# Attention scores on TensorE as three 64-row products, the two heads of a pair on the two halves of the array

## The chip, the cores and the metric

The kernel runs on one core of one Trainium2 chip. The metric is the time of one execution on the device, in microseconds (us), as the median of several runs. The profile and the trace are of one further execution. Engines are named as in the profile: PE is TensorE (PEld its weight loads), DVE is VectorE, ACT is ScalarE, POOL is GpSimd, SP is SyncE, which here only issues transfers.

## The reference

One decoder layer on x of 512 tokens by 1024 channels, in float32. What matters here is the attention part:

```
h    = rmsnorm(x, g_norm) * (1 + scale) + shift          # scale, shift, gate from silu(c) @ w_ada
proj = h @ w_in                                          # 1024 -> 4096: q k v z_attn | b_g c_g h_c z_conv
q, k = rope(q, positions), rope(k, positions)            # 8 heads of 64; halves t1, t2 of 32:
                                                         #   [t1*cos - t2*sin, t2*cos + t1*sin]
score = q @ k.T * 64 ** -0.5, causal inside blocks of 256, earlier blocks in full
y_attn = softmax(score) @ v
y_conv = b_g * conv3(c_g * h_c)
y     = concat(rmsnorm(y_attn) * silu(z_attn), rmsnorm(y_conv) * silu(z_conv)) @ w_out
out   = rmsnorm(x + gate * y, g_final)
```

With 512 tokens there are two blocks, so the selection of blocks takes every past block, and the scores are plain causal attention.

## The kernel before

**Precision.** Each float32 factor is split into a high part of fewer bits (`float32r`) and a low part, the rest. A product is three TensorE products, high by low, low by high, high by high, added in PSUM (`mm3`, lines 982 to 985). The high part is a copy on ACT, the low part a subtraction, on POOL for the weights (line 567), on DVE for q, k, v and the probabilities.

**Staging.** After the head of the program (normalised x, then q and k of head pair 0, v of all heads and C of channel group 0), the input projection goes on in 25 *units* of 128 output channels each (the list `UNITS`: H0, B0, Q1, K1, ZC0, ZA0, C1, H1, ...). A unit is 24 matmuls of 512 columns (`unit`). It writes bank n % 2 of PSUM, n its place in the list, so unit n waits until the result of unit n - 2 has been read (`emptied`): for Q and K this is the semaphore `rope_m`, which DVE raises when the products of the rotary step are done; for B it is `y_conv`, raised by `conv_out` on DVE (line 778). Between units stands the attention of one of the four head pairs p: the scores (`score`), the transposed probabilities (`transpose_probs`, ten 128x128 transposes for a head) and the product with v (`values`). Each engine has its work in an order that is written out by hand at the end of its block; semaphores tie the engines together.

**Rotary step.** The 128 channels of a Q or K unit are laid out by the host as first halves of both heads, then second halves, so `rope` on DVE is four operations: q by cos (line 730), two products of 64 rows with the crosswise sine (lines 731, 732), and the sum (line 734), which gives `rq` or `rk`.

**Scores.** For head h of the pair, `qs[:, h]` holds the 64 high rows of q and the 64 low rows side by side in 128 rows, and `kd_hi[:, h]`, `kd_lo[:, h]` hold the rows of k twice. The rows that lie in the wrong place are moved by 12 transfers a pair on the SP queue (`other_rows`, `double_q`, `double_k`). Two matmuls over 128 rows, by `kd_lo` and by `kd_hi`, then give all four partial products (lines 1090, 1091). The scores of one head take 1280 columns (four query tiles of 384, 128, 512 and 256 columns, `S_ORDER`), at banks 2 to 4 (`SB`). Both heads use the same place in turn. So `score(p, 0)` stands ahead of one unit and `score(p, 1)` behind it, and the second waits for `row_min`, DVE's last read of the first. The transposed probabilities go to banks 5 to 7 (`TB`).

**DVE around it.** `least(p, h)` (line 796) takes the scores from PSUM, adds the mask and finds the row minima (the scores are negated); ACT then takes exponentials (line 388), DVE divides by the sum (`normalise`, line 806), PE transposes, ACT copies (`pt_hi`, line 394), DVE subtracts (`probs_low`, line 812), and PE does `values`. In between DVE does the convolution (`conv_taps` lines 761 to 771, `conv_out` line 778) and the modulation vectors (line 671).

Of the kernel before, what the change touches and what calls it, by code (L numbers as in the profile page):

```python
# [4 lines left out]
F32 = mybir.dt.float32  # L5
F32R = mybir.dt.float32r
# [4 lines left out]
P = 128  # L11
# [33 lines left out]
def build(nc, x, c, pos, prm_d, ada_d, whead_d, wslots_d, gfin_d, out):  # L45
# [10 lines left out]
    SB, TB = 2 * BANK, 5 * BANK  # L56
# [6 lines left out]
    with ExitStack() as ctx:  # L63
# [35 lines left out]
        qs = sb("qs", [2, S], F32R)  # L99
# [4 lines left out]
        q_lo = sb("q_lo", [S], F32R)  # L104
        base = cursor[0]
        kd_hi = sb("kd_hi", [2, S], F32R)
        om = at("om", base, [2, BANK])
        base = cursor[0]
        kd_lo = sb("kd_lo", [2, S], F32R)
        h32 = at("h32", base, [2, S])  # L110
# [68 lines left out]
        dup_q, dup_k = sem("dup_q"), sem("dup_k")  # L179
# [46 lines left out]
        def _(sp):  # L226
# [25 lines left out]
            def other_rows(dst, src, h, done):  # L252

                for a in (0, 64):
                    to, of = a + 32 * (1 - h), a + 32 * h
                    sp.dma_start(dst[to:to + 32, h, :].bitcast(F32), src[of:of + 32, :].bitcast(F32)).then_inc(done, 16)
# [7 lines left out]
            def double_k(p):  # L264
                sp.wait_ge(qk_lo, 3 * p + 3)
                for kd in (kd_hi, kd_lo):
                    for h in range(2):
                        other_rows(kd, kd[:, h, :], h, dup_k)

            for n in range(NSLOT):  # L270
                load_raw(KT + n, wslots_d[n], D)
                if n in (5, 10, 16, 21):
                    double_q((5, 10, 16, 21).index(n))
                if n in (5, 10, 17, 22):
                    double_k((5, 10, 17, 22).index(n))
# [16 lines left out]
        def _(act):  # L292
# [58 lines left out]
            def q_high(p):  # L351
                act.wait_ge(rope_r, 2 * p + 1)
                act.wait_ge(scores, 6 * p)
                for h in range(2):
                    nc.scalar.activation(qs[:, h], rq[:, :], ACT.Copy, scale=-(HD ** -0.5)).then_inc(q_split, 1)

            def k_high(p):
                act.wait_ge(rope_r, 2 * p + 2)
                act.wait_ge(scores, 6 * p)
                for h in range(2):  # L360
                    nc.scalar.activation(kd_hi[:, h], rk[:, :], ACT.Copy).then_inc(k_split, 1)
# [116 lines left out]
            for i in range(2):  # L478
                act.wait_ge(gate_bc, i + 1)
# [826 lines left out]
```

## Time and profile before

| what | value |
|---|---|
| median of 3 runs | 290.88 us (290.7 to 291.0) |
| the profiled execution, its own time | 290.17 us |
| its span in the profile | 288.1 us |
| PE busy | 269.2 us (93% of the span), 1300 matmuls |
| PEld busy | 223.8 us (78%) |
| DVE busy | 198.9 us (69%) |
| ACT busy | 141.5 us (49%) |
| POOL busy | 113.5 us (39%) |
| granted TensorE clock | 0.993 of full over the span |

The own time of the profiled execution is 2.1 us more than its span, and 0.7 us under the median of the three runs. Busy shares are averages over the whole span; how full an engine is in one stretch has to be read from the trace. Matmul ends in the trace are modelled and overlap the next matmul, so the time that a matmul costs is read from start to start.

### The profile page before, as it was taken

To read this page: it belongs to the slowest core of one execution; us is meant where nothing else is said; L and a number is where in the kernel's file an instruction comes from. 1 tells how busy PE (TensorE), PEld (TensorE's weight loads), DVE (VectorE), ACT (ScalarE), POOL (GpSimd) and SP (SyncE) were. 2 spreads that over 40 slices of the span, in tenths; PEclk is the share of its full clock that TensorE was granted. 3 is DMA by queue.
4 is the path that set the end of the run, shared out by engine and by line. 5 is a ranking of instruction groups with operands and counts; after the bars stand their busy time and mean duration, and the time that the engine had idled before them with its cause. 6 is when DMAs were issued, how large, how long until landed. Compare 5 with 4: busy or idle time off the path is not lost.

```text
span 288.1 us, 3732 instructions
## 1 busy us (share of the span) xinstructions
PE 269.2 (93%) x1300; PEld 223.8 (78%) x1300; DVE 198.9 (69%) x348; ACT 141.5 (49%) x239; POOL 113.5 (39%) x72
## 2 busy tenths in 40 slices
PE   5479999999999999999999999999999979999990
PEld 1358888888888888888888887888888858888880
DVE  4798888699989976788998947623945621304564
ACT  5755355349058833764535254647367574302332
POOL 2400002444534433290461352055086799902321
PEclk9999999999999999999999999999999999999997
DMA  5999944394712462076352203253232518100113
GB/s 192 395 419 417 392 162 146 117 404 126 210 59 73 118 197 88 0 269 243 110 146 74 75 1 102 91 137 144 76 106 78 205 50 305 61 0 2 74 73 146
DMA packets 12260, 43.81 MB, mean 152 GB/s; under 512 B 2129, under 2 KB 2129, under 8 KB 10834
## 3 DMA queue, kind: packets, MB, share of 16 engines
q1 hardware_dynamic: 12242, 43.58, 42.6%
q8 instruction: 10, 0.16, 0.2%
q14 instruction: 8, 0.07, 0.1%
HBM read 38.33 MB, written 2.10 MB: 140 GB/s over the span
## 4 chain that ended last, share of the span: by engine, by line
PE 82%; DMA 4%; ACT 4%; POOL 3%; issue 3%; DVE 2%; SPq 1%; POOLq 0%; ACTq 0%; DVEq 0%
PE ps L983 19%; PE ps L985 18%; PE ps L984 18%; PE ps L1032 5%; DMA xt<-in_x 3%; PE ps L1116 3%; PE ps L1108 2%; PE ps L1045 2%; PE ps L1051 2%; PE ps L1043 2%; PE ps L1091 2%; PE ps L1090 2%; POOL yc_lo L583 2%; PE ps L1049 2%; PE ps L1009 1%
## 5 line engine op out<-in xcount | busy, mean ns | idle before, releaser
L567 POOL TENSOR_TENSOR w_lo<-raw,w_hi 128x1024 fp32r<-128x1024 f32 x29 | 73.7, 2549 | 124.9 <-ACT w_hi L321 124.9
L983 PE MATMUL ps<-h_lo,w_hi 128*128 128x512 f32 x200 | 78.9, 395 | 0.0
L985 PE MATMUL ps<-h_hi,w_hi 128*128 128x512 f32 x200 | 78.0, 390 | 0.0
L984 PE MATMUL ps<-h_hi,w_lo 128*128 128x512 f32 x200 | 77.9, 389 | 0.0
L985 PEld LDWEIGHTS ps<-h_hi,w_hi 128*128 128x128 f32 x200 | 37.6, 188 | 8.0
L984 PEld LDWEIGHTS ps<-h_hi,w_lo 128*128 128x128 f32 x200 | 37.6, 188 | 7.2
L983 PEld LDWEIGHTS ps<-h_lo,w_hi 128*128 128x128 f32 x200 | 37.6, 188 | 7.2
L671 DVE CUSTOM_DVE_ANT_0 mod_junk<-ada,c_bc 128x1024 f32<-128x1024 f32 x22 | 33.4, 1519 | 1.5 <-DVE acc L671 0.6
L388 ACT ACTIVATE probs<-probs,rmin 128x384 f32<-128x384 f32 (+3 forms) x32 | 17.6, 552 | 31.5 <-DVE rmin L796 31.4
L321 ACT ACTIVATE w_hi<-raw 128x1024 fp32r<-128x1024 f32 x29 | 30.1, 1050 | 4.1 <-DMA raw<-in_wslots 4.1
L806 DVE TENSOR_SCALAR probs<-probs,prec 128x384 f32<-128x384 f32 (+3 forms) x32 | 21.4, 733 | 0.3
L944 DVE TENSOR_TENSOR om<-ps,gate 128x512 f32<-128x512 f32 (+1 forms) x9 | 5.7, 629 | 20.7 <-PE ps L985 20.7
L529 ACT ACTIVATE sq_junk<-x 128x512 f32<-128x512 f32 (+1 forms) x9 | 5.3, 585 | 27.5 <-DVE x L946 27.5
L796 DVE CUSTOM_DVE_ANT_0 probs<-mask,ps 128x384 f32<-128x384 f32 (+3 forms) x32 | 13.7, 484 | 4.5 <-PE ps L1091 4.5
L343 ACT ACTIVATE h<-ps,sh,gs 128x512 f32<-128x512 f32 x8 | 6.2, 779 | 20.6 <-DVE sh L680 20.0
L983 PE MATMUL ps<-w_lo,yc_hi 128*128 128x512 f32 (+1 forms) x36 | 13.8, 382 | 1.9 <-POOL yc_lo L583 1.9
L812 DVE TENSOR_TENSOR pt_lo<-ps,pt_hi 128x1280 fp32r<-128x1280 f32 x8 | 11.9, 1487 | 4.1 <-ACT pt_hi L394 4.1
L394 ACT ACTIVATE pt_hi<-ps 128x1280 fp32r<-128x1280 f32 x8 | 9.9, 1238 | 8.3 <-PE ps L1108 8.3
L985 PE MATMUL ps<-w_hi,yc_hi 128*128 128x512 f32 (+1 forms) x36 | 13.3, 371 | 0.0
L984 PE MATMUL ps<-w_hi,yc_lo 128*128 128x512 f32 (+1 forms) x36 | 13.3, 370 | 0.0
L985 PE MATMUL ps<-wa_hi,ya_hi 128*128 128x512 f32 (+1 forms) x36 | 13.2, 367 | 0.0
L984 PE MATMUL ps<-wa_hi,ya_lo 128*128 128x512 f32 (+1 forms) x36 | 13.2, 366 | 0.0
(150 smaller groups left out, 508.5 us busy)
## 6 DMA issues: line engine op xcount, KB each, us to landing
raw<-in_wslots SPq DMA_DIRECT2D x33, 512.0 KB, 3.3
ada<-in_ada SPq DMA_DIRECT2D x11, 1024.0 KB, 9.1
raw<-in_whead SPq DMA_DIRECT2D x8, 448.0 KB, 7.2
xt<-in_x SPq DMA_DIRECT2D x4, 512.0 KB, 5.6
x<-in_x SPq DMA_DIRECT2D x4, 512.0 KB, 6.9
out<-x SPq DMA_DIRECT2D x4, 512.0 KB, 2.7
ada<-in_ada SPq DMA_DIRECT2D x2, 512.0 KB, 7.3
qs<-q_lo SPq DMA_DIRECT2D x16, 64.0 KB, 2.0
```

Of the source, the lines that this page charges most:

```text
L321: nc.scalar.activation(slot_place(n)[0], src[:, :], ACT.Copy).then_inc(s_hi, 1)
L388: nc.scalar.activation(probs[h][:, a:a + w], probs[h][:, a:a + w], ACT.Exp, scale=-1.0, bias=rmin[:, e:e + 1], accum_out=psums[:, e:e + 1] ...
L394: nc.scalar.activation(pt_hi[:, :], ps[:, TB:TB + TRI], ACT.Copy).then_inc(p_hi, 1)
L567: nc.gpsimd.tensor_tensor(lo, src[:, :], hi.bitcast(F32), ALU.subtract).then_inc(s_lo, 1)
L671: dve.tensor_tensor_reduce(mod_junk[:, :], src[:, two, :], c_rows, 1.0, 0.0, ALU.mult, ALU.add, acc[:, j, two:two + 1]).then_inc(mod_step, 1)
L796: dve.tensor_tensor_reduce(probs[h][:, a:a + w], mask[:, S - w:S], ps[:, SB + a:SB + a + w], 1.0, 3.0e38, ALU.add, ALU.min, rmin[:, e:e + ...
L806: ins = nc.vector.tensor_scalar(probs[h][:, a:a + w], probs[h][:, a:a + w], prec[:, e:e + 1], None, ALU.mult)
L812: nc.vector.tensor_tensor(pt_lo[:, :], ps[:, TB:TB + TRI], pt_hi[:, :].bitcast(F32), ALU.subtract).then_inc(p_lo, 1)
L983: nc.tensor.matmul(o, a_hi, b_lo, start=start, stop=False)
L984: nc.tensor.matmul(o, a_lo, b_hi, start=False, stop=False)
L985: return nc.tensor.matmul(o, a_hi, b_hi, start=False, stop=stop)
L1032: nc.tensor.matmul(o, a_hi, b_hi, start=(j == 0), stop=False)
```

## The change

The layout of the channels of Q and K stays as the reference has it, head 0 in rows 0 to 63 and head 1 in rows 64 to 127, so no rows need to be moved. `q2[:, 0]` and `q2[:, 1]` are the high and low parts of q, `k2` the same of k. A head's scores are three products over its 64 rows, low by high, high by low, high by high. The matmuls of the two heads alternate: rows 0 to 63 and rows 64 to 127 of the array, to different PSUM banks (2 to 4, and 5 to 7, where the transposed probabilities also go). The built program gives them arrays of 64 rows by 128 columns at row 0 and row 64, where all other matmuls have the array of 128 by 128. The 12 transfers a pair are gone, and so is the second copy of each high part on ACT and the second subtraction for k on DVE. The rotary step now takes its halves from blocks of 32 rows, four products in place of two. Both heads are scored at one place, where `score(p, 0)` was. `transpose_probs` waits until both heads' scores have been read. `gate_rows`, which uses banks 5 and 6, moves from behind unit H2 to behind `values(2, 1)`.

```diff
-    SB, TB = 2 * BANK, 5 * BANK
+    SB, TB = [2 * BANK, 5 * BANK], 5 * BANK
...
-            def double_q(p):
-                sp.wait_ge(q_split, 2 * p + 2)
-                sp.wait_ge(qk_lo, 3 * p + 1)
-                for h in range(2):
-                    other_rows(qs, q_lo, h, dup_q)
...
             def q_high(p):
                 act.wait_ge(rope_r, 2 * p + 1)
                 act.wait_ge(scores, 6 * p)
-                for h in range(2):
-                    nc.scalar.activation(qs[:, h], rq[:, :], ACT.Copy, scale=-(HD ** -0.5)).then_inc(q_split, 1)
+                nc.scalar.activation(q2[:, 0], rq[:, :], ACT.Copy, scale=-(HD ** -0.5)).then_inc(q_split, 1)
...
                 nc.vector.tensor_tensor(m1[:, :], bank(b), cos_t[:, :], ALU.mult)
-                nc.vector.tensor_tensor(m2[0:64, :], bank(b, p0=64, p1=128), sin_t[64:128, :], ALU.mult)
-                nc.vector.tensor_tensor(m2[64:128, :], bank(b, p0=0, p1=64), sin_t[0:64, :], ALU.mult).then_inc(rope_m, 1)
+                for r in range(0, P, 32):
+                    o = r ^ 32
+                    ins = nc.vector.tensor_tensor(m2[r:r + 32, :], bank(b, p0=o, p1=o + 32), sin_t[o:o + 32, :], ALU.mult)
+                ins.then_inc(rope_m, 1)
...
             def k_low(p):
-                dve.wait_ge(k_split, 2 * p + 2)
+                dve.wait_ge(k_split, p + 1)
                 dve.wait_ge(rope_r, 2 * p + 2)
-                for h in range(2):
-                    nc.vector.tensor_tensor(kd_lo[:, h], rk[:, :], kd_hi[:, h].bitcast(F32), ALU.subtract
-                                            ).then_inc(qk_lo, 1)
+                nc.vector.tensor_tensor(k2[:, 1], rk[:, :], k2[:, 0].bitcast(F32), ALU.subtract).then_inc(qk_lo, 1)
...
-            def score(p, h):
-                pe.wait_ge(dup_q, 64 * p + 64)
-                pe.wait_ge(dup_k, 128 * p + 128)
-                if h:
-                    pe.wait_ge(row_min, 8 * p + 4)
-                elif p:
+            def score(p):
+
+                pe.wait_ge(qk_lo, 2 * p + 2)
+                if p:
                     pe.wait_ge(y_attn, 2 * p)
+                    pe.wait_ge(p_lo, 2 * p)
                 else:
                     pe.wait_ge(rope_m, 2)
-                    pe.wait_ge(v_lo, 2)
+                    pe.wait_ge(v_lo, TT)
+                    pe.wait_ge(c_copy, 1)
...
-                    nc.tensor.matmul(o, qs[:, h, t], kd_lo[:, h, 0:w], start=True, stop=False)
-                    ins = nc.tensor.matmul(o, qs[:, h, t], kd_hi[:, h, 0:w], start=False, stop=True)
-                    if n:
-                        ins.then_inc(scores, 1)
+                    for term, (a, b) in enumerate(((1, 0), (0, 1), (0, 0))):
+                        for h in range(2):
+                            rows = slice(HD * h, HD * h + HD)
+                            o = ps[:, SB[h] + S_AT[i]:SB[h] + S_AT[i] + w]
+                            ins = nc.tensor.matmul(o, q2[rows, a, t], k2[rows, b, 0:w], start=(term == 0), stop=(term == 2))
+                            if n and term == 2:
+                                ins.then_inc(scores, 1)
 
             def transpose_probs(p, h):
                 pe.wait_ge(p_norm, 2 * p + h + 1)
-                if p == 0 and h == 0:
-                    pe.wait_ge(v_lo, TT)
-                    pe.wait_ge(c_copy, 1)
-                elif h == 0:
-                    pe.wait_ge(p_lo, 2 * p)
-                    if p == 2:
-                        pe.wait_ge(gate_ok, 2)
+                pe.wait_ge(row_min, 8 * p + 8)
...
             unit("Q1")
-            score(0, 0)
+            score(0)
             unit("K1")
-            score(0, 1)
             unit("ZC0")
             transpose_probs(0, 0)
```

PE's order before, from the last matmul of unit Q1 to the first of K1: eight matmuls for head 0 (`ps` is PSUM, `qs`, `kd_lo`, `kd_hi` the split factors).

```order
L985 MATMUL ps<-h_hi,w_hi_53 128x512
L1090 MATMUL ps<-kd_lo,qs 128x384 [waits rope_m,v_lo,dup_k,dup_q]
L1091 MATMUL ps<-kd_hi,qs 128x384
L1090 MATMUL ps<-kd_lo,qs 128x128
L1091 MATMUL ps<-kd_hi,qs 128x128
L1090 MATMUL ps<-kd_lo,qs 128x512
L1091 MATMUL ps<-kd_hi,qs 128x512
L1090 MATMUL ps<-kd_lo,qs 128x256
L1091 MATMUL ps<-kd_hi,qs 128x256
L983 MATMUL ps<-h_lo,w_hi_54 128x512 [waits y_conv,s_lo]
```

The same place in the change: 24 matmuls of 64 rows for both heads, and the waits for the transfers are one for the low parts.

```order
L957 MATMUL ps<-h_hi,w_hi_53 128x512
L1067 MATMUL ps<-k_81,q_74 128x384 [waits v_lo,c_copy,rope_m,qk_lo]
L1067 MATMUL ps<-k_81,q_74 128x384 x5
L1067 MATMUL ps<-k_81,q_74 128x128 x6
L1067 MATMUL ps<-k_81,q_74 128x512 x6
L1067 MATMUL ps<-k_81,q_74 128x256 x6
L955 MATMUL ps<-h_lo,w_hi_54 128x512 [waits y_conv,s_lo]
```

Head 0's scores moved nowhere; head 1's eight matmuls, which stood behind K1, are gone from there. Unit K1 still waits for `y_conv`.

DVE's order before, `conv_out(0)`, the rotary step of Q1 and the start of `least(0, 0)` (`m_70`, `m_71` are the two addends of the rotary step; an ISA row is the min operation or its read-out):

```order
L778 TENSOR_TENSOR yc<-yc,ps 128x512 [waits unit_out,tap_ok]
L730 TENSOR_TENSOR m_70<-ps,cos_t 128x512 [waits q_split,unit_out]
L731 TENSOR_TENSOR m_71<-ps,sin_t 64x512
L732 TENSOR_TENSOR m_71<-ps,sin_t 64x512
L734 TENSOR_TENSOR rq<-m_70,m_71 128x512 [waits rope_m]
L796 ISA probs_92,rmin<-mask,ps 128x384 [waits scores,mask_ok]
```

The same in the change:

```order
L750 TENSOR_TENSOR yc<-yc,ps 128x512 [waits unit_out,tap_ok]
L703 TENSOR_TENSOR m_70<-ps,cos_t 128x512 [waits q_split,unit_out]
L706 TENSOR_TENSOR m_71<-ps,sin_t 32x512 x4
L709 TENSOR_TENSOR rq<-m_70,m_71 128x512 [waits rope_m]
L768 ISA probs_90,rmin<-mask,ps 128x384 [waits scores,mask_ok]
```

Two instructions of 64 rows have become four of 32 rows of the same length, at the same place; the order of DVE's steps is otherwise kept.

PE's order before, from the end of unit ZC0 over the transposes of head 0 to unit ZA0:

```order
L984 MATMUL ps<-h_hi,w_lo_61 128x512
L985 MATMUL ps<-h_hi,w_hi_55 128x512
L1108 MATMUL ps<-ident,probs_92 128x128 [waits c_copy,v_lo,p_norm]
L1108 MATMUL ps<-ident,probs_92 128x128 x9
L983 MATMUL ps<-h_lo,w_hi_56 128x512 [waits rope_m,s_lo]
```

And in the change:

```order
L956 MATMUL ps<-h_hi,w_lo_61 128x512
L957 MATMUL ps<-h_hi,w_hi_55 128x512
L1078 MATMUL ps<-ident,probs_90 128x128 [waits row_min,p_norm]
L1078 MATMUL ps<-ident,probs_90 128x128 x9
L955 MATMUL ps<-h_lo,w_hi_56 128x512 [waits rope_m,s_lo]
```

The transposes of head 0 now wait for `row_min` of both heads.

## Rows read from the trace of the kernel before

**Rows 1.** The page: busy time of each engine over the span.
```profile
PE 269.2 (93%) x1300; PEld 223.8 (78%) x1300; DVE 198.9 (69%) x348; ACT 141.5 (49%) x239; POOL 113.5 (39%) x72
```

**Rows 2.** The waits of PE, the longest behind the program's first 20 us.
```profile
PE ps L983 <- POOL yc_lo L583: 1.9, 4, 1.0
```

**Rows 3.** Windows: PE, PEld, DVE, ACT, POOL busy us in one stretch, clock, DMA.
```profile
60.00:80.00 20.00, 20.00 (x93) 16.67 (x92) 19.53 (x21) 7.88 (x11) 9.07 (x4) 1.00 0.70 236
```

**Rows 4.** Timeline of PE around unit K1: start us, duration us, instruction.
```profile
76.67 0.33 PE L1090 MATMUL ps<-kd_lo,qs 128*128 128x384 f32 x1
...
77.01 0.22 PE L1090 MATMUL ps<-kd_lo,qs 128*128 128x128 f32 x1
77.07 0.27 PE L1091 MATMUL ps<-kd_hi,qs 128*128 128x128 f32 x1
...
77.94 0.40 PE L983 MATMUL ps<-h_lo,w_hi 128*128 128x512 f32 x1
...
83.39 0.33 PE L1090 MATMUL ps<-kd_lo,qs 128*128 128x384 f32 x1
```

**Rows 5.** Timeline of DVE, 57 to 78 us.
```profile
57.83 0.69 DVE L730 TENSOR_TENSOR m<-ps,cos_t 128x512 f32<-128x512 f32 x1 [2.26 <-PE ps L1038]
58.53 0.69 DVE L731 TENSOR_TENSOR m<-ps,sin_t 64x512 f32<-64x512 f32 x1
...
59.95 1.93 DVE L734 TENSOR_TENSOR rq<-m,m 128x512 f32<-128x512 f32 x1
...
66.62 1.29 DVE L748 TENSOR_TENSOR kd_lo<-rk,kd_hi 128x512 fp32r<-128x512 f32 x2
...
71.31 5.57 DVE L771 SCALAR_TENSOR_TENSOR yc<-u,prm,yc 128x512 f32<-128x512 f32 x2
76.91 0.69 DVE L778 TENSOR_TENSOR yc<-yc,ps 128x512 f32<-128x512 f32 x1
77.51 0.69 DVE L730 TENSOR_TENSOR m<-ps,cos_t 128x512 f32<-128x512 f32 x1
```

**Rows 6.** Timeline of POOL, 58 to 77 us.
```profile
58.94 2.40 POOL L567 TENSOR_TENSOR w_lo<-raw,w_hi 128x1024 fp32r<-128x1024 f32 x1 [0.68 <-ACT w_hi L321]
68.58 7.74 POOL L567 TENSOR_TENSOR w_lo<-raw,w_hi 128x1024 fp32r<-128x1024 f32 x3 [7.25 <-ACT w_hi L321]
```

**Rows 7.** Timeline of DVE, 88 to 96 us.
```profile
88.35 0.68 DVE L730 TENSOR_TENSOR m<-ps,cos_t 128x512 f32<-128x512 f32 x1
...
94.42 1.48 DVE L812 TENSOR_TENSOR pt_lo<-ps,pt_hi 128x1280 fp32r<-128x1280 f32 x1
```

**Rows 8.** Timeline of PE, 90 to 97 us.
```profile
90.12 1.25 PE L1108 MATMUL ps<-ident,probs 128*128 128x128 f32 x10
...
96.71 0.39 PE L1116 MATMUL ps<-pt_lo,v 128*128 128x512 f32 x1
```

**Rows 9.** Timeline of DVE in head pair 1, 123 to 136 us.
```profile
123.37 6.25 DVE L806 TENSOR_SCALAR probs<-probs,prec 128x384 f32<-128x384 f32 x4
...
134.08 1.48 DVE L812 TENSOR_TENSOR pt_lo<-ps,pt_hi 128x1280 fp32r<-128x1280 f32 x1
```

**Rows 10.** Timeline of PE, `values(1, 0)`.
```profile
136.72 0.39 PE L1116 MATMUL ps<-pt_lo,v 128*128 128x512 f32 x1
```

**Rows 11.** Timeline of PE and ACT in head pair 2, 171 to 179 us.
```profile
171.97 1.25 PE L1108 MATMUL ps<-ident,probs 128*128 128x128 f32 x10
...
175.02 1.15 ACT L355 ACTIVATE qs<-rq 128x512 fp32r<-128x512 f32 x2 [5.28 <-DVE rq L734]
...
178.88 0.50 PE L1116 MATMUL ps<-pt_lo,v 128*128 128x512 f32 x1 [0.17 <-DVE pt_lo L812]
```

**Rows 12.** Timeline of POOL and ACT behind pair 3's scores, 209 to 218 us.
```profile
209.42 4.85 POOL L567 TENSOR_TENSOR w_lo<-raw,w_hi 128x1024 fp32r<-128x1024 f32 x2 [7.09 <-ACT w_hi L321]
...
216.62 1.26 ACT L421 ACTIVATE diag<-ident,rsy 128x128 f32<-128x128 f32 x4
```

**Rows 13.** The page: transfers by tile, count, size, us to landing.
```profile
qs<-q_lo SPq DMA_DIRECT2D x16, 64.0 KB, 2.0
```

More of the change, by code:

```diff
@@ L103, in build @@
         sin_k, cos_k = at("sin_k", base + 8192, [TT, P]), at("cos_k", base + 10240, [TT, P])
[L104 removed]
         base = cursor[0]
[L106 removed]
+        k2 = sb("k2", [2, S], F32R)
         om = at("om", base, [2, BANK])
         base = cursor[0]
[L109 to L110 removed]
+        h32 = sb("h32", [2, S])
         diag = at("diag", base, [TT, P])
@@ L359, in k_high @@
                 act.wait_ge(scores, 6 * p)
-                for h in range(2):
-                    nc.scalar.activation(kd_hi[:, h], rk[:, :], ACT.Copy).then_inc(k_split, 1)
+                nc.scalar.activation(k2[:, 0], rk[:, :], ACT.Copy).then_inc(k_split, 1)
             def value_high(m):
@@ L477, in _ @@
             exponents(2, 1)
-            for i in range(2):
-                act.wait_ge(gate_bc, i + 1)
-                nc.scalar.activation(gate[:, i * BANK:(i + 1) * BANK], bank(5 + i), ACT.Copy).then_inc(gate_ok, 1)
             square_y(0, 2)
@@ L491, in _ @@
             other_half(2, 1)
+            for i in range(2):
+                act.wait_ge(gate_bc, i + 1)
+                nc.scalar.activation(gate[:, i * BANK:(i + 1) * BANK], bank(5 + i), ACT.Copy).then_inc(gate_ok, 1)
             square_y(1, 2)
@@ L736, in q_low @@
             def q_low(p):
[L737 removed]
+                dve.wait_ge(q_split, p + 1)
                 dve.wait_ge(rope_r, 2 * p + 1)
[L739 to L741 removed]
+                nc.vector.scalar_tensor_tensor(out=q2[:, 1], in0=rq[:, :], scalar=-(HD ** -0.5),
+                                               in1=q2[:, 0].bitcast(F32), op0=ALU.mult, op1=ALU.subtract
                                                ).then_inc(qk_lo, 1)
             def k_low(p):
[L745 removed]
+                dve.wait_ge(k_split, p + 1)
                 dve.wait_ge(rope_r, 2 * p + 2)
[L747 to L749 removed]
+                nc.vector.tensor_tensor(k2[:, 1], rk[:, :], k2[:, 0].bitcast(F32), ALU.subtract).then_inc(qk_lo, 1)
             def value_low(m):
@@ L1177, in _ @@
             unit("H1")
-            score(1, 0)
+            score(1)
             unit("B1")
-            score(1, 1)
             unit("ZC1")
@@ L1189, in _ @@
             unit("C2")
-            score(2, 0)
+            score(2)
             unit("H2")
-            score(2, 1)
-            gate_rows()
             unit("B2")
@@ L1201, in _ @@
             values(2, 1)
+            gate_rows()
             unit("C3")
-            score(3, 0)
+            score(3)
             unit("H3")
-            score(3, 1)
             unit("B3")
@@ L1258, in cols @@
         n = np.arange(P)
-        if kind in "QK":
-            n = (n // 32 % 2) * 64 + (n // 64) * 32 + n % 32
         return start[kind] + p * P + n
@@ L1282, in host_layout @@
     i = np.arange(P)
-    prm[:, C_SIGN] = np.where(i < 64, 1.0, -1.0)
+    prm[:, C_SIGN] = np.where(i // 32 % 2 == 0, 1.0, -1.0)
     prm[:, C_INVF:C_INVF + 32] = (10000.0 ** (-np.arange(32) / 32)).astype(np.float32)
```

33 lines of the change are left out of this document (8 added, 25 removed).

## The prediction

> **What bounds the kernel now.** I read the page first. PE is busy 93% of the span, and no other engine above 69% [rows 1]. A busy matmul row can hide idle pipeline, so I went to the waits of PE next: behind the first 20 us there is almost nothing, 1.9 us for `yc_lo` near the end [rows 2] and 0.17 us at one `values` [rows 11]. PE's own timeline says what work costs, read from start to start: unit K1 runs from 77.94 to 83.39, 5.45 us for 24 matmuls of 512 columns [rows 4], so 0.227 us each, or 0.443 ns a column. The clock is granted in full there [rows 3]. So PE's work in sequence is the time, and a microsecond taken from it counts, as does one in which it waits for the first time. Last I looked at who is close behind. In the stretch 60 to 80 us DVE is busy 19.53 of 20 us [rows 3]. The average of 69% hides that: in head pair 0 DVE is as full as PE. That is the stretch from which I read the DVE part of the change.
>
> **The scores on PE.** Head 0's eight matmuls take from 76.67 to 77.94, 1.27 us [rows 4], so 2.54 us a pair, in two places. One product of one head streams 1280 columns, 0.57 us. After, a pair has six such products. No row shows two halves of the array at work, so I bound it. Streamed side by side, three times 0.57 is 1.70. A matmul of 128 columns needs 0.06 us when only its columns count (77.01 to 77.07 [rows 4]), and 0.11 with its weights ahead of it (ten transposes take 1.25 with the last one's tail of about 0.2 [rows 8]), so the three narrow ones add 0.15: 1.9 us. If weights are loaded one after the other, 24 loads at 0.11 are 2.7 us, and 3.0 if the array also runs empty at the change of its form on both sides (a matmul row lasts 0.40 where the next starts 0.23 later [rows 4], so 0.17 each time). If the halves don't overlap at all, it is 6 x 0.57 = 3.4 plus six times 0.05, 3.7 us, and up to 4.0 with the change of form; I take 3.8 for that case. I take 2.4 us, between the two overlapped cases, since neither row is of this kind. The array's own gain is then 0.14 us a pair, 0.6 us in all, of 290.
>
> The Trainium skill, TensorEngine Tiling (Array Packing), section Key Properties, says that different tiles load weights and multiply in parallel, and that a change of tiling mode drains TensorE. By it the figure would be near 1.9 plus two drains, 2.2 us. No run here shows either yet.
>
> **The rotary step on DVE.** Its products of 64 rows last 0.69 us, as long as the one of 128 rows, and start 0.70 apart [rows 5]. So rows don't count, and four products of 32 rows cost 1.4 us more than two of 64, eight times: 11.3 us of DVE. What goes: one `kd_lo` a pair, 0.6 us [rows 5], and on ACT one of each two copies of q and of k, about 0.55 us each time (1.15 for two [rows 11]). The 12 transfers a pair are off the path already (landed in 2.0 us, no PE wait names them) [rows 2, 13]; I cost their removal at nothing.
>
> **Head pair 0.** Rope Q0: its sum took 1.93 us instead of 0.69, since POOL ran a subtraction until 61.34 [rows 5, 6]. Now the sum starts at 61.35, when that is over, so Q0 ends only 0.2 later. Rope K0 adds 1.4: 1.6. One k subtraction less: 1.0. ACT, with one k copy less, is also 1.0 late, so the three POOL subtractions of 68.58 to 76.32 move with it and hold up `conv_taps(0)` as before (two operations in 5.57 us, over just behind the last of the three) [rows 5, 6]. `conv_out(0)` then ends at 78.6 (before 76.91 + 0.69 = 77.60). K1 waits for it, but the scores now end at 76.67 + 2.4 = 79.1, so nothing is lost there. Rope Q1 adds 1.4, so both `least` of pair 0 are 2.4 late. The second ends at 90.9 instead of 88.4, where K1's rotary step follows it [rows 7].
>
> PE meanwhile: K1 and ZC0 from 79.1 to 90.0. Before, the transposes began at 90.12 [rows 8]; they needed only head 0's probabilities. Now they wait for `row_min` of both heads, until 90.9 (wait 0.9), and end 1.1 later, at 92.0. ZA0 needs bank 1, read by K1's rotary products: these start at 90.8 and take five times 0.705, until 94.3 (before 88.35 + 3 x 0.70 = 90.5, ahead of PE's 91.2). So PE waits 2.3 us there, and `values(0, 0)` starts at 94.3 + 5.45 = 99.8 instead of 96.71 [rows 8]. Its input `pt_lo` was ready at 94.42 + 1.48 = 95.9 [rows 7] and is 2.4 + 1.4 later, 99.7, just in time. Pair 0: **+3.1 us**, and this hardly depends on the 2.4, since DVE sets it. Behind this DVE has idle time and is in step again.
>
> **Head pair 1.** The scores save 0.14. B1's end, for which `conv_out(1)` waits, comes 2.4 - 1.27 = 1.13 later after the scores' start than before. The chain conv_out, normalise, least, normalise (the last one 6.25 us, slowed by POOL [rows 9]) carries this on to rope Q2, which adds 1.4: `pt_lo` at 135.56 + 2.5 = 138.1 in the old frame [rows 9], while PE is there at 136.72 - 0.14 = 136.6 [rows 10]. Wait 1.5. Pair 1: **+1.4 us**.
>
> **Head pair 2.** `gate_rows` is moved, not changed; its ACT copies go behind a unit. Nothing waits for either, since C3 (5.45 us) lies between it and the scores. From the end of Q3 to `values(2, 0)` PE took 178.88 - 171.97 = 6.91 us with a wait of 0.17 [rows 11]: rope Q3, ACT's copies of q (1.15), `pt_hi`, `pt_lo` in a chain. This chain gets 1.4 for the rotary step and loses 0.55 for one copy. So +0.85, less 0.14 on the scores: **+0.7 us**.
>
> **Head pair 3.** +1.13 ahead of H3, -1.27 behind it. DVE is not in front here. Behind it `y_squares` comes 1.27 earlier, but POOL is on weights until 209.42 + 4.85 = 214.27, then makes `rsy`; ACT's `diag` (216.62) stood behind it and a copy [rows 12] and gains about 1.1. That stretch leads to the `yc_lo` wait [rows 2]. Net **0**.
>
> **Sum.** 3.1 + 1.4 + 0.7 + 0 = +5.2 us, of which PE's own work is -0.6 and the waits are the rest, 5.8. Against the profiled execution's 290.17 this is 295.4; that execution lies 0.7 under the median, so I predict **296.1 us**.
>
> **The rivals.** *One: the halves don't overlap.* Scores 3.8 us a pair. Pair 0 is set by DVE as before, the other three get 1.4 more each: 296.1 + 4.2 = 300.3. For it speaks that no row shows overlap; against it, that the program asks for separate halves. *Two, on the other side: DVE's extra time is swallowed.* It happened to Q0 on paper, where 1.4 became 0.2 because the sum waited for POOL anyhow. If the operations of 5.57 and 6.25 us take up the lateness in the same way, DVE's chain of pair 0 must stay under the slack of 1.7 us (88.4 against 90.12) to cost nothing. Then only pair 2's 0.9 is left, and with scores at 1.9 us the sum is 290.9 - 4 x 0.64 + 0.9 = 289.2. Against it: the POOL work is started by ACT copies that follow DVE, so it shifts along. *Three: more of it.* Where a DVE operation with two operands in SBUF falls into a POOL subtraction it costs up to 2.5 us more; the sum of rope K1 will lie close to one. One or two of these give 298 to 300. *Four: no change*, if Two happens by half: the waits of pair 0 shrink to the saving, 291.
>
> **How the numbers follow.** Chances: my forecast's mechanism, including Three, 0.74 (its own range 292.9 to 299.8: scores 1.9 to 3.0 us give -1.5 to +1.8, and one POOL collision more or less in pair 0 or 1 gives -1.7 to +1.9); One 0.11; Two 0.10; Four 0.05. Less than 0.2% can't be told from no change in a measurement of this kernel. Slower is then 0.74 + 0.11 = 0.85, same 0.05, faster 0.10. The range: below, it leaves out Two and Four; above, half of One. 292.3 to 300.2.
>
> **What would show it.** Each score block of the changed kernel from its first matmul to the next unit: 2.4 us (1.9, 2.7 or 3.8 tell the bounds apart). PE rows with waits for DVE: transposes of pair 0 by `row_min` (0.9), ZA0 by the rotary products (2.3), `values(1, 0)` (1.5) and `values(2, 0)` (1.0) by `pt_lo`. DVE busy up by about 9 us, ACT down by 5, no 64 KB transfers. I am wrong if PE has no new waits, or if the four products of 32 rows last less than 0.69 us each.

## The result and the profile after

The changed kernel takes 303.25 us (median; 300.12 to 303.51) where the kernel before takes 290.94 us in the same call (290.7 to 291.39). The ratio is 1.040, with a 95% interval of 1.033 to 1.047. That is +12.3 us, where +5.2 was forecast, and 3 us above the top of the range. The profiled execution took 303.39 us. Its span, 301.6 us, is 13.5 us longer than the span before; the accounts below are made from these two spans. Two single executions in the runs below, one of 547 us of the kernel that comes last and one of 1526 us of the kernel before, are left out of the ranges and ratios.

The page of the changed kernel, busy time of each engine (answers to [rows 1]) and the granted clock in 40 slices of the span:

```profile
PE 273.5 (91%) x1332; PEld 224.8 (75%) x1332; DVE 209.2 (69%) x360; ACT 137.7 (46%) x231; POOL 112.6 (37%) x72
...
PEclk9999999999998899999999999799999997999997
```

DVE is up by 10.3 us and ACT down by 3.8; about 9 and 5 were forecast. The second row is what the forecast had no term for. In it the clock dips in slices 13 and 14 (90 to 106 us), 26 (from 188 us), 34 (from 249 us) and 40; before, it dips in slice 40 alone. The mean granted clock is 0.976 here, 0.993 before.

The waits of PE, in us in total, times, longest (answers to [rows 2], where only the wait for `yc_lo` stood):

```profile
PE ps L1086 <- DVE pt_lo L784: 5.5, 2, 3.9
...
PE ps L955 <- DVE m L706: 2.1, 1, 2.1
...
PE ps L955 <- POOL yc_lo L556: 1.9, 4, 1.0
...
PE ps L1078 <- DVE rmin L768: 1.2, 1, 1.2
```

The four waits of the forecast are there: 0.9, 2.3, 1.5 and 1.0 were expected, and 1.19, 2.12, 1.55 and 3.91 came. Three hit within 0.3 us. The fourth, at `values(2, 0)`, is 2.9 us longer. The wait for `yc_lo` is as long as before.

**The scores.** Timeline of PE at the first score block (answers to [rows 4]):

```profile
76.62 0.39 PE L957 MATMUL ps<-h_hi,w_hi 128*128 128x512 f32 x1
76.94 2.19 PE L1067 MATMUL ps<-k,q 64*128 64x384 f32 x24
79.13 0.47 PE L955 MATMUL ps<-h_lo,w_hi 128*128 128x512 f32 x1
79.44 0.39 PE L956 MATMUL ps<-h_hi,w_lo 128*128 128x512 f32 x1
```

The 24 matmuls for both heads take 2.19 us. Both ends cost a little more: the last matmul of unit Q1 starts 0.32 us ahead of the scores, where 0.227 is usual, and the first of K1 is 0.31 ahead of the next. The first can be the change of the array's form, since ahead of the ten transposes, where the form stays, the distance is 0.23. The second can't be told from something else: behind the ten transposes it is 0.31 as well. The other three blocks take 2.12 us. With both ends counted a pair costs 2.36 us here and 2.32 at the other three, where before it cost 2 x 1.27 [rows 4]. So the 2.4 of the forecast was right, and PE's own gain is about 0.2 us a pair, 0.8 in all.

**Head pair 0.** The timeline of DVE and of POOL at the rotary step of K1 (answers to [rows 7]):

```profile
91.25 0.68 DVE L703 TENSOR_TENSOR m<-ps,cos_t 128x512 f32<-128x512 f32 x1
91.94 2.79 DVE L706 TENSOR_TENSOR m<-ps,sin_t 32x512 f32<-32x512 f32 x4
...
93.52 2.37 POOL L540 TENSOR_TENSOR w_lo<-raw,w_hi 128x1024 fp32r<-128x1024 f32 x1 [3.98 <-ACT w_hi L296]
...
94.76 1.68 DVE L709 TENSOR_TENSOR rk<-m,m 128x512 f32<-128x512 f32 x1
```

The four products take 2.79 us, 0.70 each. The sum behind them takes 1.68 instead of 0.69 while POOL is at work, until 95.89. That is the collision that rival Three feared, at the place that it named. But it is no new loss. In the kernel before, the same piece of POOL work (90.63 to 93.43) fell on the `normalise` behind the sum:

```profile
91.28 3.22 DVE L806 TENSOR_SCALAR probs<-probs,prec 128x384 f32<-128x384 f32 x4
```

In the change this `normalise` takes 1.28 us. So the collision cost 1.9 us of DVE before and costs 1.0 now, and `pt_lo` starts 3.45 us later than before (97.87 against 94.42) where the forecast had 3.8. The timeline of PE (answers to [rows 8]):

```profile
91.47 1.28 PE L1078 MATMUL ps<-ident,probs 128*128 128x128 f32 x10 [1.19 <-DVE rmin L768]
...
94.87 0.47 PE L955 MATMUL ps<-h_lo,w_hi 128*128 128x512 f32 x1 [2.12 <-DVE m L706]
...
96.36 0.63 PE L955 MATMUL ps<-h_lo,w_hi 128*128 128x512 f32 x1
96.78 0.63 PE L956 MATMUL ps<-h_hi,w_lo 128*128 128x512 f32 x1
...
102.02 0.39 PE L1086 MATMUL ps<-pt_lo,v 128*128 128x512 f32 x1
```

Read the starts. ZA0 begins at 94.87 (forecast 94.3). From 96.36 to 99.34 its matmuls last 0.63 us and start 0.42 apart, where 0.39 and 0.227 are usual [rows 4]. The unit takes 7.15 us instead of 5.5, and `values(0, 0)` starts at 102.02; 99.8 was forecast. PE waited 1.19 us, did ten transposes, and waited 2.12 us just before. Windows of the same stretch, and of two others (from:to, length, busy us of PE, PEld, DVE, ACT, POOL, granted clock, DMA share, GB/s):

```profile
94.00:98.00 4.00, 3.13 (x10) 2.57 (x11) 3.89 (x9) 3.99 (x6) 1.89 (x1) 0.78 0.27 63
188.00:192.00 4.00, 4.00 (x20) 3.86 (x19) 3.88 (x7) 0.94 (x2) 1.38 (x1) 0.57 0.38 128
250.00:254.00 4.00, 4.00 (x12) 3.20 (x12) 0.95 (x2) 2.45 (x6) 3.63 (x3) 0.59 0.85 263
```

At the full clock each would show 1.00; the means of 0.78, 0.57 and 0.59 say that for a part of each window, in the last two most of it, the clock is at its lower level, 1.2 GHz instead of 2.4. There are three such stretches: behind the wait of ZA0, behind the wait of `values(2, 0)`, and at 250 us, behind the four short waits for `yc_lo` and a run of matmuls of one column (1.75 us of them, 248.20 to 249.95).

**Head pair 2.** The wait of 3.91 us leads back to DVE, from there to POOL, and from there to ACT. Timeline of ACT, POOL and DVE:

```profile
175.19 0.62 ACT L384 ACTIVATE sq<-yc 128x512 f32<-128x512 f32 x1
...
175.53 4.54 DVE L778 TENSOR_SCALAR probs<-probs,prec 128x384 f32<-128x384 f32 x4
...
175.71 1.04 ACT L296 ACTIVATE w_hi<-raw 128x1024 fp32r<-128x1024 f32 x1
...
175.88 1.29 POOL L546 TENSOR_TENSOR sqsum<-sqsum,sq 128x512 f32<-128x512 f32 x1 [6.13 <-ACT sq L384]
...
177.12 2.40 POOL L540 TENSOR_TENSOR w_lo<-raw,w_hi 128x1024 fp32r<-128x1024 f32 x1
...
179.99 0.68 DVE L703 TENSOR_TENSOR m<-ps,cos_t 128x512 f32<-128x512 f32 x1
```

And the same instructions in the kernel before:

```profile
167.21 1.06 ACT L480 ACTIVATE gate<-ps 128x512 f32<-128x512 f32 x2
...
167.61 1.27 DVE L806 TENSOR_SCALAR probs<-probs,prec 128x384 f32<-128x384 f32 x4
...
168.69 1.05 ACT L321 ACTIVATE w_hi<-raw 128x1024 fp32r<-128x1024 f32 x1
...
168.87 1.30 POOL L573 TENSOR_TENSOR sqsum<-sqsum,sq 128x512 f32<-128x512 f32 x1 [7.09 <-ACT sq L411]
```

`normalise(2, 1)` (four operations) takes 1.27 us before and 4.54 after. Before, ACT's two copies for `gate` stood ahead of `square_y(0, 2)` and of the weight copy of slot 18, the two that release POOL. POOL began at 168.87, and `normalise` was over at 168.88. After, with the gate copies moved away, POOL begins at 175.88, 0.35 us behind the start of `normalise`, and works through it until 179.52. The rotary step of Q3 then starts at 179.99, though PE had ended Q3 at 176.90. PE behind it (answers to [rows 11]):

```profile
176.90 1.25 PE L1078 MATMUL ps<-ident,probs 128*128 128x128 f32 x10
...
187.56 0.50 PE L1086 MATMUL ps<-pt_lo,v 128*128 128x512 f32 x1 [3.91 <-DVE pt_lo L784]
...
189.26 2.35 PE L1078 MATMUL ps<-ident,probs 128*128 128x128 f32 x10
```

From the end of Q3 to `values(2, 0)` it is 10.66 us (6.91 before). The ten transposes behind it take 2.01 us from start to start instead of 1.04: again the lower clock.

**The sum.** The waits of PE grew by about 8.6 us (1.2 + 2.1, 1.55, 3.75). The three stretches at the lower clock cost about 4.7 us (1.6, 1.6, 1.5: each is the stretch's length less that of the same work before). PE's own work is 0.8 us less. That is 12.5 of the 13.5 us; the remaining 1.0 I did not trace.

### The profile page after: what moved, and what is told of

Its sections match the earlier page's. It is cut to its first block, busy times and chain, and to the rows that moved or that the text cites. A ratio compares the mean times of both kernels' runs of the same rounds, so it can differ in the third digit from the quotient of the medians.

```text
span 301.6 us, 3749 instructions
## 1 busy us (share of the span) xinstructions
PE 273.5 (91%) x1332; PEld 224.8 (75%) x1332; DVE 209.2 (69%) x360; ACT 137.7 (46%) x231; POOL 112.6 (37%) x72
## 4 chain that ended last, share of the span: by engine, by line
PE 59%; DVE 21%; issue 5%; ACT 5%; DMA 4%; POOL 3%; SPq 1%; POOLq 0%; DVEq 0%; ACTq 0%
PE ps L955 13%; PE ps L956 12%; PE ps L957 12%; DVE m L706 5%; PE ps L1004 5%; DVE probs L778 4%; DVE yc L743 3%; PE ps L1086 3%; DMA xt<-in_x 3%; PE ps L1067 2%; PE ps L1017 2%; PE ps L1023 2%; PE ps L1078 2%; ACT probs L361 2%; POOL yc_lo L556 2%
## 5 line engine op out<-in xcount | busy, mean ns | idle before, releaser
L540 POOL TENSOR_TENSOR w_lo<-raw,w_hi 128x1024 fp32r<-128x1024 f32 x29 | 72.7, 2517 | 137.7 <-ACT w_hi L296 137.7
L955 PE MATMUL ps<-h_lo,w_hi 128*128 128x512 f32 x200 | 80.3, 402 | 2.1 <-DVE m L706 2.1
L778 DVE TENSOR_SCALAR probs<-probs,prec 128x384 f32<-128x384 f32 (+3 forms) x32 | 22.8, 775 | 0.3
L706 DVE TENSOR_TENSOR m<-ps,sin_t 32x512 f32<-32x512 f32 x32 | 22.0, 687 | 0.4
L955 PE MATMUL ps<-w_lo,yc_hi 128*128 128x512 f32 (+1 forms) x36 | 14.5, 404 | 1.9 <-POOL yc_lo L556 1.9
L1086 PE MATMUL ps<-pt_lo,v 128*128 128x512 f32 (+3 forms) x32 | 10.1, 324 | 5.5 <-DVE pt_lo L784 5.5
```

The lines of the kernel that those rows point to most:

```text
L540: nc.gpsimd.tensor_tensor(lo, src[:, :], hi.bitcast(F32), ALU.subtract).then_inc(s_lo, 1)
L706: ins = nc.vector.tensor_tensor(m2[r:r + 32, :], bank(b, p0=o, p1=o + 32), sin_t[o:o + 32, :], ALU.mult)
L778: ins = nc.vector.tensor_scalar(probs[h][:, a:a + w], probs[h][:, a:a + w], prec[:, e:e + 1], None, ALU.mult)
L955: nc.tensor.matmul(o, a_hi, b_lo, start=start, stop=False)
L1086: ins = nc.tensor.matmul(bank(2 + h, j * P, BANK), v2[:, j, 2 * p + h, :], pt[:, T_AT[j]:T_AT[j] + S - j * P], start=(j == 0 and n == 0), ...
```

## The experiments

Two things had to be told apart: what caused the lateness of DVE (the rotary step, or the rule that both heads are read before the transposes), and why it cost twice the forecast (ACT's order in pair 2, and the clock). The kernel before took 291.01 to 291.08 us in the calls of these runs.

### The rotary step alone

The changed kernel with the two products of 64 rows of before. It leaves out the right rotation: the halves are taken from the other head's rows.

```diff
-                for r in range(0, P, 32):
-                    o = r ^ 32
-                    ins = nc.vector.tensor_tensor(m2[r:r + 32, :], bank(b, p0=o, p1=o + 32), sin_t[o:o + 32, :], ALU.mult)
-                ins.then_inc(rope_m, 1)
+                nc.vector.tensor_tensor(m2[0:64, :], bank(b, p0=64, p1=128), sin_t[64:128, :], ALU.mult)
+                nc.vector.tensor_tensor(m2[64:128, :], bank(b, p0=0, p1=64), sin_t[0:64, :], ALU.mult).then_inc(rope_m, 1)
```

> The changed kernel with the rotary step's two products of 64 rows of before in place of the four of 32 (with the new channel layout they take the wrong halves, so this leaves out the right rotation). Theory A, the loss comes from 11 us more on DVE: PE's new waits in head pairs 0 and 1 go, and with them the stretches at half clock; 289.5 to 292.5 us. Rival B, the loss comes from scoring both heads at one place and from the transposes that wait for both: it stays at 298 or more. PE should show no wait for DVE at unit ZA0, where it was 2.1 us.

Measured: 292.91 us (291.62 to 293.78), ratio 1.0055 [1.0032, 1.0077], span 292.0 us. Its waits of PE:

```profile
PE ps L1084 <- DVE pt_lo L782: 2.1, 1, 2.1
PE ps L953 <- POOL yc_lo L556: 2.0, 4, 1.1
```

The time is 0.4 us above the range that was expected. The waits for `row_min`, for `m` and of pair 1 are gone. One is left, 2.1 us at `values(2, 0)`; `normalise(2, 1)` still takes 4.54 us here (168.81 to 173.35). So without the four products of 32 rows 10.3 of the 12.3 us are gone (303.25 less 292.91). The profiled execution, at 293.78 the longest of ten, also has the stretch at the lower clock near the end (7.19 us for a piece of work that takes 5.68 at the full clock). The ten times lie in two groups, and the mean granted clock goes with them: four from 291.6 to 292.1 us at 0.994 or 0.995, six from 292.8 to 293.8 us at 0.987 to 0.989. So the clock falls in some executions and not in others; where it fell in those without a trace isn't shown.

The converse: the kernel before with its two products cut in four.

```diff
-                nc.vector.tensor_tensor(m2[0:64, :], bank(b, p0=64, p1=128), sin_t[64:128, :], ALU.mult)
-                nc.vector.tensor_tensor(m2[64:128, :], bank(b, p0=0, p1=64), sin_t[0:64, :], ALU.mult).then_inc(rope_m, 1)
+                for r in range(0, P, 32):
+                    o = (r + 64) % P
+                    ins = nc.vector.tensor_tensor(m2[r:r + 32, :], bank(b, p0=o, p1=o + 32), sin_t[o:o + 32, :], ALU.mult)
+                ins.then_inc(rope_m, 1)
```

> The kernel before, with each of the two products of 64 rows in the rotary step split into two of 32 rows; nothing else, the output is the same. Theory A: DVE alone makes most of the loss, 298 to 303 us, with waits of PE for conv_out at unit K1, for the rotary products and for pt_lo. Rival B: 291 to 293, since transposes need only one head there.

Measured: 299.01 us (297.59 to 300.42), ratio 1.0273 [1.0217, 1.0329], span 298.5 us. The three largest waits of PE that are new ("issue" stands where the profile shows no releaser):

```profile
PE ps L1092 <- issue: 2.2, 2, 1.9
...
PE ps L1118 <- DVE pt_lo L814: 1.9, 2, 1.6
...
PE ps L985 <- DVE m L733: 1.8, 1, 1.8
```

Nothing else is changed here, and the time rises by 8.0 us. The waits for `m` and `pt_lo` are of the same kinds as in the changed kernel, and ZA0 takes 7.17 us, at the lower clock, as there. So a loss of this kind doesn't need the new scores. But the 8.0 are not simply a part of the 12.3: the 2.2 us at L1092 are waits at two score blocks, and the changed kernel has no like of them. The longer one, 1.92 us, ends at 159.97, when the transfers of the rows of k have landed: their issue runs from 153.48 to 158.42, and each lands about 2.0 us after its own. A late DVE brings the transfers onto the path, which the change no longer has. And the granted clock differs between the executions: two at 0.995 and 0.996 took 297.6 and 297.7 us, two at 0.988 took 300.3 and 300.4.

### Both heads before the transposes

The rival for pair 0: the new wait for both heads' minima does the harm. In the kernel before, that wait alone:

```diff
                 pe.wait_ge(p_norm, 2 * p + h + 1)
+                pe.wait_ge(row_min, 8 * p + 8)
```

> The kernel before, with transpose_probs waiting for the row minima of both heads, as in the change. The second minima are ready 1.7 us ahead of PE there, so Theory A expects no change, 290.9; rival B (this wait is a main cause) 293 or more.

Measured: 290.79 us (290.24 to 292.82), ratio 1.0004 [0.9977, 1.0032], span 288.2 us. Nothing. Before, both minima were there before PE came. The rival falls: the wait of 1.19 us for `rmin` is DVE's lateness, shown at this place. In the changed kernel the rule does decide where PE waits: head 0's probabilities are ready at 89.69 there, ahead of PE (90.12). But ZA0 starts when DVE lets it, at 94.87, so without the rule the same time would have been waited there. The kernel before with the products cut has the late DVE without the rule, and it shows this: no wait at the transposes (92.56), then 1.81 us at ZA0.

### The halves of the array

The changed kernel with both heads on rows 0 to 63 (head 1 gets head 0's scores).

```diff
-                            rows = slice(HD * h, HD * h + HD)
+                            rows = slice(0, HD)
```

> The changed kernel with both heads' scores taken from rows 0 to 63, so that every score matmul is on the same half of the array (head 1 gets head 0's scores). If the halves overlap in the changed kernel, a score block goes from 2.19 us to 3.7 to 3.9 and the time up by 2 to 5 us, to 305 to 308 (less than 4 times 1.6, since PE waits for DVE in three pairs anyway). If they don't overlap and the loads are the limit, the block and the time stay.

Measured: 305.09 us (304.43 to 306.39), ratio 1.0487 [1.0448, 1.0527], span 302.4 us. The first score block in the timeline of PE:

```profile
76.81 4.10 PE L1067 MATMUL ps<-k,q 64*128 64x384 f32 x24
80.85 0.50 PE L955 MATMUL ps<-h_lo,w_hi 128*128 128x512 f32 x1
```

From start to start that is 4.04 us, where the two halves take 2.12 to 2.19: 1.9 times as long. Four blocks are 7.6 us longer, yet the time is only 1.8 us more than that of the changed kernel: PE comes later to the places at which it waited for DVE, and those waits shrink (for `rmin` from 1.19 us to none, at ZA0 from 2.12 to 1.46, at `values(2, 0)` from 3.91 to 2.34). Those are 3.4 us. About 3 more are the clock's: of the three stretches at the lower level this execution has one, behind `values(2, 0)`; ZA0 and the stretch near the end ran at the full clock.

### ACT's order in pair 2

The changed kernel, with slot 18 and `square_y(0, 2)` moved behind what `values(2, 0)` needs:

```diff
-            square_y(0, 2)
-            slot(18)
             q_high(3)
             probs_high(2, 0)
+            slot(18)
+            square_y(0, 2)
             slot(19)
```

> The changed kernel with ACT's square of y_conv 2 and copy of weight slot 18 put behind q_high(3) and probs_high(2, 0). In the changed kernel these two came a microsecond earlier than before, since the gate copies no longer stand ahead of them, and the POOL work that they start falls on normalise(2, 1) (4.54 us instead of 1.27). If that is what made the wait at values(2, 0) 3.9 us, it falls to about 1 and the half clock behind it goes: 298.5 to 300.5 us. If the wait is from the rotary step alone, 303.

Measured: 298.87 us (296.69 to 300.03), ratio 1.0286 [1.0230, 1.0342], span 294.8 us. `normalise(2, 1)` in its timeline:

```profile
173.30 1.27 DVE L778 TENSOR_SCALAR probs<-probs,prec 128x384 f32<-128x384 f32 x4
```

The waits of PE:

```profile
PE ps L1086 <- DVE pt_lo L784: 2.6, 2, 1.6
...
PE ps L955 <- DVE m L706: 2.1, 1, 2.1
...
PE ps L955 <- POOL w_lo L540: 1.0, 1, 1.0
```

And the window at ZA0, with the columns as above:

```profile
94.00:98.00 4.00, 3.73 (x17) 3.12 (x18) 3.90 (x8) 3.85 (x6) 1.34 (x2) 1.00 0.38 130
```

`normalise` is back at 1.27 us, and the wait at `values(2, 0)` is 1.07, just what the prediction said for this place. The edit is worth 4.4 us, although it brings a wait of 1.0 us of its own, for the weights of slot 18, which are late now. The wait at `values(2, 0)` is 2.8 us shorter, and in the profiled execution the transposes behind it run at the full clock. So this chain of four engines (ACT's order, POOL's start, `normalise`, rope Q3) is what made the term of pair 2 too small. And ZA0 waited 2.13 us here too, but the clock stayed at 1.00 and the unit took 5.53 us: the same wait doesn't always cost the clock. The executions of this kernel are spread over 3.3 us, from 296.69 at a mean clock of 0.993 to 300.03 at 0.984, and one stretch such as that of ZA0 is half of that.

### Filling the waits

If the lower clock comes from PE having been idle, work in the gap should keep it up, and take nothing, since PE waits there anyway. Unread products are put ahead of ZA0 and of `values(2, 0)`:

```diff
+            def filler(count):
+                for _ in range(count):
+                    nc.tensor.matmul(bank(2), h_hi[:, 0, 0:P], h_hi[:, 1], start=True, stop=True)
...
             transpose_probs(0, 0)
+            filler(8)
             unit("ZA0")
...
             unit("K3")
+            filler(14)
             values(2, 0)
```

> The changed kernel with matmuls of 512 columns that nothing reads: 8 between the first transposes and unit ZA0, 14 between unit K3 and values(2, 0), where PE waits 2.1 and 3.9 us. If the idle time is what makes the granted clock fall behind these two places, both stretches stay at full clock and the time falls by about 3 us, to 300; the third stretch, near the end, stays. If the clock falls for another reason, the time stays at 303 or grows.

Measured: 299.36 us (298.80 to 299.92), ratio 1.0292 [1.0257, 1.0326], span 297.0 us, mean clock 0.996. The timeline of PE at ZA0:

```profile
92.43 2.09 PE L1136 MATMUL ps<-h_hi 128*128 128x512 f32 x8
94.80 0.47 PE L955 MATMUL ps<-h_lo,w_hi 128*128 128x512 f32 x1 [0.28 <-DVE m L706]
...
100.34 0.39 PE L1086 MATMUL ps<-pt_lo,v 128*128 128x512 f32 x1
```

ZA0 starts at 94.80, as without the filler (94.87), since DVE sets that. But the unit takes 5.54 us instead of 7.15, and `values(0, 0)` is at 100.34 instead of 102.02. With DVE as late as before, and 22 useless matmuls more in the place of waits, the kernel is 3.9 us faster. The stretch at 250 us was expected to stay; it is at the full clock as well, though nothing was filled there. The ten transposes behind `values(2, 0)` take 1.03 us, as before the change. What the medians give back, 3.9 us, stands beside the 4.7 of my account, and the two profiled executions differ by 4.6 (303.39 and 298.80; two of the other three of this kernel have a mean clock of 0.987 or 0.988 again). So the clock's part is shown, and its size to within a microsecond.

The last run of this kind puts both causes right. It is the changed kernel with ACT's order of pair 2 mended, here with a wait for `normalise` ahead of slot 18, and eight filler products at ZA0:

```diff
             exponents(2, 1)
-            square_y(0, 2)
+            act.wait_ge(p_norm, 6)
             slot(18)
             q_high(3)
             probs_high(2, 0)
+            square_y(0, 2)
             slot(19)
...
             transpose_probs(0, 0)
+            filler(8)
             unit("ZA0")
```

> The changed kernel with both mends: slot 18 held as in e8, and 8 matmuls that nothing reads ahead of unit ZA0. What is left are the waits from the rotary step alone at full clock: 1.1 + 2.1 in pair 0, 1.5 in pair 1, about 1 in pair 2; 295.5 to 297.5 us, which is what the prediction's sum should have met. If it stays above 299, something else is in the loss.

Measured: 296.07 us (295.36 to 296.53), ratio 1.0171 [1.0133, 1.0209], span 294.7 us. Its waits of PE for DVE:

```profile
PE ps L1087 <- DVE pt_lo L785: 2.6, 2, 1.6
...
PE ps L1079 <- DVE rmin L769: 1.2, 1, 1.2
...
PE ps L956 <- DVE m L707: 0.3, 1, 0.3
```

These are the waits of the prediction (with the filler in the place of most of the wait for `m`), and the time is that of the prediction's sum, 296.1. That it fits to 0.1 us is luck in part: the four executions spread over 1.2 us, and the profiled one has a span 6.6 us above that of before, where the sum has 5.2.

### The new scores without the new rotary step

If the array's halves are a gain and the products of 32 rows a loss, the two can be parted. This kernel keeps the layout and the rotary step of before, scores both heads as the change does, and sorts the rows with transfers, eight a pair of 128 KB where before had 12 of 64 KB:

```diff
+            def regroup(dst, src, p, k, done):
+                sp.wait_ge(qk_lo, 2 * p + 1 + k)
+                if p:
+                    sp.wait_ge(scores, 6 * p)
+                for of, to in ((0, 0), (32, 64), (64, 32), (96, 96)):
+                    sp.dma_start(dst[to:to + 32, :, :].bitcast(F32), src[of:of + 32, :, :].bitcast(F32)).then_inc(done, 16)
```

> Scores as in the change, on two halves of the array, but with the channel layout and the rotary step of before (two products of 64 rows); the 32-row blocks are put in the new order by 8 transfers a pair, high and low parts together, behind the splits. Output as the reference. Theory A: PE does 0.6 us less than before, DVE 0.6 us a pair less, and there are no new waits except that at values(2, 0); 289.5 to 292. Rival B: 296 or more. If a transfer of 128 KB is late at scores(0), PE waits there, up to 2 us more.

Measured: 293.10 us (291.62 to 294.17), ratio 1.0074 [1.0047, 1.0101], span 290.9 us. The first score block takes 2.19 us. `normalise(2, 1)` in the timeline:

```profile
167.75 4.54 DVE L790 TENSOR_SCALAR probs<-probs,prec 128x384 f32<-128x384 f32 x4
```

The wait of PE for DVE that is left:

```profile
PE ps L1099 <- DVE pt_lo L796: 2.0, 1, 2.0
```

The page's row of the transfers of q (count, size, us to landing):

```profile
q<-qt SPq DMA_DIRECT2D x16, 128.0 KB, 2.3
```

Slower than before, by 2.0 us, and above the range that was expected: pair 2's `normalise` takes 4.54 us here, too. `gate_rows` is moved as in the change, and the rotary step is that of before, so this collision doesn't need the products of 32 rows. The piece of work near the end took 7.23 us, at the lower clock. The clock fits the other part of the 2.0 us: eight of the ten executions have a mean clock of 0.987 to 0.989, and the two at 0.994 and 0.995 took 291.62 and 291.95 us. Here is the same kernel with ACT's order of pair 2 mended:

```diff
             exponents(2, 1)
-            square_y(0, 2)
+            act.wait_ge(p_norm, 6)
             slot(18)
             q_high(3)
             probs_high(2, 0)
+            square_y(0, 2)
             slot(19)
```

> e7_halves_by_dma with ACT's copy of weight slot 18 held until normalise(2, 1) is done and the square of y_conv 2 behind probs_high(2, 0). In e7 normalise(2, 1) took 4.54 us and values(2, 0) waited 2.0 us. If POOL's work on DVE's operands is the cause, normalise takes 1.3, the wait goes under 0.3 us and the time falls by 2 us, to 290.5 to 291.3, level with the kernel before. If the cause is another, it stays at 293.

Measured: 290.44 us (289.59 to 290.80), beside 291.03 for the kernel before; ratio 0.9977 [0.9958, 0.9995], span 287.7 us, mean clock 0.994. `normalise(2, 1)` in the timeline:

```profile
168.08 1.27 DVE L791 TENSOR_SCALAR probs<-probs,prec 128x384 f32<-128x384 f32 x4
```

The only wait of PE behind the first 20 us:

```profile
PE ps L968 <- POOL yc_lo L570: 2.0, 4, 1.1
```

And a window over pair 2:

```profile
160.00:200.00 40.00, 39.99 (x213) 33.54 (x212) 22.12 (x45) 20.14 (x35) 14.79 (x8) 1.00 0.30 93
```

PE is busy 39.99 of 40 us. This version is clearly faster than the changed kernel, and all but level with the kernel before: 0.23% less, where the prediction called less than 0.2% too little to tell from no change, and an interval that ends at 0.9995. PE's own gain in the scores, 0.8 us, would fit this difference; the time alone doesn't show that it is the cause. The array's halves are worth no more than that here.

## Why the prediction was wrong

**What bounds the kernel** was right: PE's sequence is the time, and DVE is close behind in pair 0. The kernel before with the products cut moved by 8.0 us with nothing changed in PE's own work.

**The score block** (2.4 us) was right: 2.36 and 2.32 with both ends counted. The Trainium skill, TensorEngine Tiling (Array Packing), section Key Properties, says that tiles load weights and multiply in parallel and that a change of mode drains TensorE; the runs agree on the first, with 2.12 to 2.19 us against 4.04 on one half, and fit the second with about 0.1 us ahead of a block; what stands behind it isn't told apart. Rival One is out.

**The rotary step** was right in mechanism and price: 0.70 us a product of 32 rows, DVE up by 10.3 us. Both new waits of pair 0 (0.9 and 2.3 forecast, 1.19 and 2.12 measured) and that of pair 1 (1.5, 1.55) came where the prediction put them. Rival Two is out: DVE's time isn't swallowed. The removed transfers, costed at nothing, have no wait of PE in the kernel before either.

Two terms failed, and they account for the miss. The sum gave 295.4 us for a profiled execution, and 303.39 were measured, 8.0 more: 2.9 are the wait of head pair 2, 4.7 the clock, and 0.4 are left. Each alone would have stayed near the forecast: with the first mended the median is 298.87, with the clock held up 299.36, both inside the range.

**Head pair 2** is the step of the sum that failed, and there rival Three had the right mechanism, but looked for its loss at rope K1. "`gate_rows` is moved, not changed; its ACT copies go behind a unit." It goes on that nothing waits for either. PE's part of it is true. What I didn't look at is what stood behind those copies on ACT's queue: a square and a weight copy, each of which releases an operation on POOL, and DVE's `normalise` runs at that time. The copies had been holding POOL off it. The term was +0.7 us; the wait at its end alone grew by 3.75 us. With the order mended it is 1.07, with 1.0 forecast.

**A missing term: the clock**, and by size the larger one. The prediction took each wait at its length and all work behind it at the full clock, which it had read from one stretch, 60 to 80 us [rows 3]; a fall behind a wait stood at nothing, without a reason. Three stretches of the changed kernel, two of them right behind new waits, ran at 1.2 GHz in part, for about 1.5 us more each. The dips behind the two waits went when these were filled with useless matmuls, and in the other runs a dip comes and goes. The Trainium skill, TensorE: Matmul & The Clock Gate, Part 1, says that activity releases the throttle, idleness brings it back, and that the same kernel differs in this from run to run. The trace agrees: a wait of 2.12 us at ZA0 was followed by a unit of 7.15 us in one kernel, and one of 2.13 by a unit of 5.53 us in another.

**Open.** What decides at 250 us. Every kernel here has the same four waits for `yc_lo` there (1.0 and three of 0.3 us). In the profiled executions the clock falls behind them in the changed kernel, with the products of 64 rows, and with the scores by transfers, and holds in the kernel before and in the others. But this isn't a property of the kernel. In one call 6 of 19 executions of the kernel before have a mean clock of 0.987 to 0.989 and take 291.5 to 292.8 us, and 13 have 0.991 to 0.994 and take 290.2 to 291.2. These runs don't show why, nor where the clock fell in the executions without a trace. It is 1.5 us of the 13.5. For the same reason the times of kernels with such waits can't be forecast to a microsecond: the changed kernel itself has one execution at 300.12 us, at a mean clock of 0.988, and three above 303, at 0.976 or 0.977.

## What to carry over

On DVE a product of 32 rows by 512 columns takes 0.70 us from start to start, as one of 64 or 128 rows does. A layout that saves transfers but cuts an elementwise step in more pieces moves work from queues with room onto the engine that is nearly full: here 0.8 us gained on PE and some 10 lost.

When work is moved on a queue, list what stands behind it there and what each of those releases on other engines. Here two copies that nobody waited for had held a sum and a weight subtraction of POOL off `normalise`.

Count a first wait of some microseconds on PE as its length and, with a chance, about 1.5 us more for the clock behind it. If the wait can't be removed, matmuls that nobody reads can be put in it: eight of them ahead of ZA0 moved its start by nothing (94.80 us against 94.87).

## What the runs showed of the hardware

- Pairs of 64-row fp32r products on the two halves of the array: 24 matmuls with 7680 columns in all, and as many weight loads, take 2.12 to 2.19 us, against 4.04 us on one half.
- DVE's `normalise` (four operations, one tensor operand in SBUF, result in SBUF) takes 1.27 us alone, 4.54 us with a sum and a subtraction of POOL beside it, and 6.25 us in pair 1 [rows 9]. Most of the time for which POOL worked beside a DVE operation is lost to it: 3.3 of 3.6 us in pair 2, 5.0 of 5.9 in pair 1 before, 1.9 of 2.2 at `normalise(0, 1)` before, 1.0 of 1.1 at the sum of rope K1. Rival Three had such a collision only for operations with two operands in SBUF, though the prediction itself had put the 6.25 us down to POOL. The Trainium skill, GPSIMD Engine Reference, section Specifications, says that the SBUF interfaces are shared with VectorE, with contention for its instructions "in a 2-port perf mode or with two SBUF inputs"; the trace agrees that the two contend (4.54 us against 1.27), and no run here shows in which mode `normalise` ran.
- The mean granted clock differs between executions of one kernel, and the time with it: 0.987 to 0.989 against 0.991 to 0.994 in the kernel before, with 291.5 to 292.8 against 290.2 to 291.2 us.
